# In every expert of a mixture-of-experts decoder step, the gather of the next expert's rows is issued behind the down product instead of in front of it

## The reference, cut to what matters

```
e_flat = expert.reshape(n_assign)            # 2 experts of each of the 264 tokens
x_pad  = zeros(...).at[dest].set(hf[tok_sorted])
def expert_block(xb, e):
    return (silu(xb @ w_gate[e]) * (xb @ w_up[e])) @ w_down[e]     # 2048 -> 512 -> 2048
y = y_pad[dest] * w_sorted
out = segment_sum(y, tok_sorted)
```

## Time and profile before

| | |
|---|---|
| median of 3 runs | 1639.27 us (1638.75 to 1639.69) |
| the profiled execution | span of 1635.1 us from its first to its last instruction; it has no time of its own beside that, and 4.2 us lie between the span and the median of the runs |
| TensorE's matmuls busy | 1355.8 us, 83% of the span |
| VectorE, ScalarE, GpSimd busy | 293.3, 226.8 and 75.6 us |
| mean granted TensorE clock | 0.924 of full speed |
| HBM read | 514.32 MB, 330 GB/s over the span |
| chain that ended last | DMA 47%, TensorE 23% of the span |

### The profile page before, as it was taken

How to read it: one execution, slowest core, us unless ns; L and a number is a source line. 1 busy time by engine, 2 the same in 40 slices (tenths; PEclk the granted TensorE clock), 3 DMA queues, 4 the chain that set the end, 5 groups by cost and what they waited for, 6 DMA issues and landing times.

```text
span 1635.1 us, 21890 instructions
## 1 busy us (share of the span) xinstructions
PE 1355.8 (83%) x9071; PEld 754.3 (46%) x9072; DVE 293.3 (18%) x819; ACT 226.8 (14%) x512; POOL 75.6 (5%) x160
## 2 busy tenths in 40 slices
PE   9999999999999798777777767767677677676997
PEld 7878888888887333222222222222222222223543
DVE  4312321156512301010000100100100000103212
ACT  3101221223211111000000000000000000002303
POOL 1000000200040000000000000000000000000000
PEclk9999999999999799888978988888988887987999
DMA  9555333578886899999999999999999999996352
GB/s 314 176 178 182 129 129 120 185 255 319 266 297 253 357 427 427 428 428 428 428 428 429 428 428 429 427 429 428 428 429 429 428 428 418 425 392 211 105 178 80
DMA packets 106372, 535.71 MB, mean 328 GB/s; under 512 B 13988, under 2 KB 36712, under 8 KB 79945
## 3 DMA queue, kind: packets, MB, share of 16 engines
q1 hardware_dynamic: 101584, 530.56, 81.1%
q0 software_dynamic: 2560, 4.34, 0.7%
q10 hardware_dynamic: 2176, 0.09, 0.1%
HBM read 514.32 MB, written 24.62 MB: 330 GB/s over the span
## 4 chain that ended last, share of the span: by engine, by line
DMA 47%; PE 23%; DVE 1%; ACT 0%; issue 0%; SPq 0%; POOLq 0%; DVEq 0%
DMA raw<-in_w_up 38%; DMA more<-in_w_up 8%; PE ps L2081 7%; PE ps L1854 7%; PE ps L154 4%; PE ps L1292 1%; PE ps L2098 1%; PE ps L1874 1%; PE ps L1333 1%; PE ps L1863 1%; PE ps L1834 1%; DMA more<-expert_rows 0%; DMA expert_rows<-hT,si 0%; PE ps L1493 0%; PE ps L2070 0%
## 5 line engine op out<-in xcount | busy, mean ns | idle before, releaser
L1854 PE MATMUL ps<-raw,hT 128*32 128x512 f32 x1504 | 232.7, 752 | 158.7 <-DMA raw<-in_w_gate 95.6
L154 PE MATMUL ps<-hT,raw 128*128 128x264 f32 x1280 | 291.4, 387 | 0.0
L154 PEld LDWEIGHTS ps<-hT,raw 128*128 128x128 f32 x1280 | 240.8, 190 | 41.9 <-issue 1.5
L1854 PEld LDWEIGHTS ps<-raw,hT 128*32 128x32 f32 x1504 | 46.6, 125 | 310.7 <-DMA raw<-in_w_gate 124.5
L154 PE MATMUL ps<-mixT,raw 128*128 128x264 f32 x640 | 145.5, 387 | 2.4 <-PEq L839 1.5
L1874 PE MATMUL ps<-more,hid 128*32 128x512 f32 x1024 | 125.6, 620 | 21.1 <-DMA more<-in_w_down 21.0
L154 PEld LDWEIGHTS ps<-mixT,raw 128*128 128x128 f32 x640 | 120.8, 190 | 25.0 <-issue 3.9
L1863 PEld LDWEIGHTS ps<-fold,hT 128*128 128x128 f32 x512 | 69.6, 208 | 97.6 <-ACT hT L1768 61.7
L2081 PE MATMUL ps<-raw,more 128*128 128x512 f32 x256 | 114.1, 602 | 0.0
L1810 DVE TENSOR_TENSOR hid<-ps,sig 128x128 f32<-128x128 f32 x32 | 9.3, 291 | 573.3 <-PE ps L1863 573.3
L1292 PE MATMUL ps<-x_res,mine 128*32 128x512 f32 (+1 forms) x792 | 105.5, 649 | 2.2 <-DVE mine L1282 2.2
(11 more groups left out here) (389 smaller groups left out, 793.4 us busy)
## 6 DMA issues: line engine op xcount, KB each, us to landing
more<-in_w_down SPq DMA_DIRECT2D x64, 2048.0 KB, 26.3
raw<-in_w_gate SPq DMA_DIRECT2D x62, 2048.0 KB, 26.3
more<-in_w_up SPq DMA_DIRECT2D x32, 2048.0 KB
raw<-in_w_up SPq DMA_DIRECT2D x32, 2048.0 KB, 26.6
raw<-in_w_in SPq DMA_DIRECT2D x44, 1024.0 KB, 5.1
raw<-in_w_out SPq DMA_DIRECT2D x16, 1024.0 KB, 8.5
raw<-in_w_ple_gate SPq DMA_DIRECT2D x16, 1024.0 KB, 5.0
x_res<-in_state_mlstm_C SPq DMA_DIRECT2D x8, 1024.0 KB, 8.4
```

Source lines behind the costliest of these rows:

```text
L154: return nc.tensor.matmul(ps[:, j, 0:NT], core.raw[:, q % NCH, k * GW + j * P:k * GW + (j + 1) * P], xT[:, core.groups[g].k0 + c * CK + k, ...
L1854: last = nc.tensor.matmul(ps[own, (GATE, UP)[m], :], xT[:, k, i * SLOTS:(i + 1) * SLOTS], weights, start=(i == 0 and k < 4), stop=(i == EI ...
```

## The change

In `expert`, TensorE's order for one expert, two calls change places. It holds for all 32 experts. No instruction is added or removed, and no other engine's order is touched.

```
                 folded(0, n)
                 project(1, 1, n)
                 folded(1, n)
+                down(n)
                 gather_slots(core, pe, rt, q, p * (NE + 1) + e + 1)
-                down(n)
                 x_turn(p * (NE + 1) + e + 1)
```

## The result

In the first comparison the changed kernel took 1645.57 us (median of 4 runs, 1640.18 to 1648.58) and the kernel before 1639.48 (1638.75 to 1639.95): a ratio of 1.0038, 95% interval 1.0019 to 1.0056. Repeated with twelve runs against 35 it was 1.0021 (1.0006 to 1.0037), medians 1642.66 and 1639.28. So the change costs 0.2 to 0.4%. The forecast was 1640.5 with a range up to 1643.0, and "no difference" with a chance of 0.92. It was wrong. Rival 3 named what happened; its 1642 to 1643.8 us holds the median of the longer series, not the first one.

What follows compares the result with a forecast made beforehand. The weight stream by DMA was taken as the bound, 29.97 us per expert. Start 0, loop 0, last expert -0.05 + 1.3 made 1639.27 + 1.25 = 1640.5 us, range 1637.4 to 1643.0.

Steps and rivals of the forecast that it cites:

- no difference: Whole kernel: time within 0.2%, 3.3 us, of the kernel before; chance 0.92.
- Rival 3: Start, seventh and eleventh load: stream runs dry, 1.3 to 2.8 us lost, 1642 to 1643.8 us; chance 0.12.
- Loop, +0: Expert loop: TensorE makes good its lag in two chunks, beat stays 29.97 us per expert; cost 0.
- The lateness of gate 0's slot: Loop: gate 0's slot given back 3.6 us later; its load has 26 to 28 us and needs 8.0.
- Last expert, -0.05 + 1.3: Last expert: down 1 still waits for its chunk, gaining 0.05 us; half clock there adds 1.3 us.
- rival 1: Last expert: down 1's chunk comes in time, tail gains the whole 2.15 us, 1637.1 us; chance 0.05.
- The two pauses, 0.75 and 0.8 us: Each expert: TensorE waits 0.75 us ahead of down for `hid`, 0.8 us ahead of the turn for ScalarE's copy.
- The start, "0, by a hair": Experts 0 to 3: TensorE 1.55 us later per expert, loads still in time; cost 0, bounds 0 and 1.5 us.
- The margins of 2.1 and 3.3 us: Start: queue ahead of the seventh load 2.1 us, eleventh 3.3 us, against lateness of 1.55 and 3.1 us.
- The signs that the prediction named: Wrong if beat not 29.97 us, DMA share under 0.9 between 575 and 605 us, or last scatter over 2 us away.
- The first reading of the earlier trace: Slices 15 to 36: DMA 9 tenths or more busy, TensorE at 6 to 8 tenths, so TensorE has time over.
- The range: Whole kernel: 1637.4 to 1643.0 us, from rival 1's edge to rival 3's middle.

Runs made afterwards that it cites:

- the kernel with the pieces later: New order everywhere, the four pieces of the embedding's projection behind experts 2 to 5 instead of 0 to 3, against the kernel before: 1637.7 us, ratio 0.9991.
- the pauses filled: New order everywhere, in experts 0 to 3 one unread 128 x 384 product in each new pause, against the kernel before: 1640.7 us, ratio 1.0005.

## Why the prediction was wrong, step by step

- **Loop, +0: right.** Beat 29.97 us, gate 0 released by VectorE, 8.5 us behind the landing; new order in the loop alone costs nothing that the times show. (The lateness of gate 0's slot, 3.6 us, is 3.8 by the prediction's own terms; nothing hangs on it.)
- **Last expert, -0.05 + 1.3: right in kind, two thirds in size.** Down 1 waits for its landing, so the whole gain of taking the gather out of the chain (rival 1) was never there. A down 1 partly at half clock cost 0.6 to 0.9 us in four profiles and 1.4 in one; in the kernel with the pieces later it had full clock.
- **The two pauses, 0.75 and 0.8 us: right** (0.71 and 0.81).
- **The start, "0, by a hair": this is the step that failed.** Its two terms were both mis-sized, the lateness and the margin. The lateness was taken at full clock, with the words "TensorE is packed there and at full clock" against rival 3. That was true of the kernel before, whose gather stood in the pause; the change takes that cover away. The prediction counted what the pause costs in waiting and, although it priced half clock for the last expert, not what it costs in clock in the first four. In the changed kernel's two profiles half clock brought the seventh load's lateness from 1.55 to 3.1 us, and the eleventh's from 3.1 to 4.6 and 7.7 (in the second profile 0.5 of each is from the gate chunks, ahead of the pauses). With the pauses filled the loss is 0.4 us, in an execution with quick gate chunks; without it is 2.8 and 5.5.
- **The margins of 2.1 and 3.3 us** were too wide: the eleventh load's was 1.2 to 2.4 us, and 1.8 us more per expert at full clock lose 1.6 us of stream already. So the start would not have been free at full clock either. The signs that the prediction named for its being wrong came: a DMA share of 0.85 at 579 to 583 us, and a last scatter 3.4 us later.
- **The first reading of the earlier trace rows passed over the place.** It says that TensorE falls to 6 to 8 tenths in all slices from the 15th on. The 15th, 572 to 613 us, shows 9 for TensorE as well as for DMA: it is experts 1 and 2, where the two dips lie.
- **Rival 3** had the mechanism, the place, the loads and the direction; its upper price of 2.8 us was half of what the worse execution lost. By its own terms its times are 1641.8 to 1643.3 us and not 1642 to 1643.8.
- **The range** was built on a spread of 1.2 us that more runs didn't bear out, and on a profiled execution called ordinary that was some 2 us under the median. The four first runs of the changed kernel happened to lie high as well; twelve more bring the loss to 0.2%.

The Trainium skill's rule on the clock (page "TensorE: Matmul & The Clock Gate", section "HAM oscillation — how this bites in real kernels"), cited in the prediction for waits on DMA at the end, speaks in that section of matmul bursts between DMA waits. The trace shows the same effect behind waits of 0.7 us for ScalarE and VectorE, with a short fold between them, in a stretch that was otherwise packed. At the end the prediction read its rows loosely: gate 1's wait of 3.45 us is longer than the 1.92 us of products ahead of it, but up 1's 1.93 us of waiting followed 3.0 us of products (up 0 and the fold) and it still ran at half clock. So only gate 1 is the case that the section describes.

## What to carry to other kernels

A stream that is the bound may still depend on the slowest stretch of the compute engine: look for the stage where the ring of slots has least in it (here the first three experts), and compute there each load's slack, the time that it may be late before the stream runs dry, from the dips of GB/s and not from the landing times alone. An instruction that stands in a short wait may be worth more than its time, since it also keeps TensorE's clock; before it is moved, price the pause twice, as waiting and as clock. And compare stages between two marks of one profile when totals scatter by more than the effect.

## What the runs showed that was not expected

- Half clock behind pauses of only 0.7 us: 0.72 of waiting, 1.13 of eight short products, 0.71 of waiting, and 32 instructions of the down product take 5.34 instead of 3.64 us (1.2 in place of 2.4 GHz for a part of it). It is not so behind every such pair of pauses: expert 1 in the same execution, and expert 0 in the second one, took 3.64. With 0.89 us of a useless product in the second pause they took 3.64 in experts 0, 1 and 2 alike.
- The same kernel loses 2.8 or 5.5 us of stream in two executions, depending on where in the first experts the clock is low.
- 17 to 26 useless products ahead of expert 0 shorten the way from the first gather to the first slot given back from 12.0 us (11.8 to 13.1 in the profiles without them) to 8.7, in three of four profiles; in the fourth it is 10.5.
